# Gathering a block's tokens as 128 half rows instead of 64 whole rows, in a two-layer mixture-of-experts trunk

## What is computed

```
def expert_block(args):
    e, tok, g = args
    xb = ht[tok]
    hid = jax.nn.silu(xb @ w1[e]) * (xb @ w3[e])
    return (hid @ w2[e]) * g[:, None].astype(ht.dtype)
```

## Time and profile before

| | |
|---|---|
| median of 3 executions | 1592.72 us (1591.69 to 1592.96) |
| profiled execution | 1593.22 us |
| its span, first to last instruction | 1591.4 us |
| PE busy | 1360.1 us (85%) |
| DVE, ACT, POOL busy | 757.1, 508.5, 125.4 us |
| HBM read, written | 312.06 MB, 30.24 MB |
| expert stage of layer 0 | from 474 to about 872 us |
| expert stage of layer 1 | from 1239 to about 1555 us |

### The profile page before, as it was taken

One profiled execution on the slowest core, in us unless ns is written; L12 is line 12 of the kernel. 1 busy time (PEld: TensorE's weight loads), 2 busy tenths in 40 slices (PEclk: granted clock), 3 DMA queues, 4 the chain that ended last, 5 costly groups with the idle time before them and its releaser, 6 DMA issues. The chain is left out here.

```text
span 1591.4 us, 22877 instructions
## 1 busy us (share of the span) xinstructions
PE 1360.1 (85%) x6778; PEld 638.4 (40%) x6779; DVE 757.1 (48%) x1405; ACT 508.5 (32%) x783; POOL 125.4 (8%) x176
## 2 busy tenths in 40 slices
PE   4799998469968899999998399799897779989980
PEld 2555563224433333333332244388643323323330
DVE  2699999955764221222211542366547322232215
ACT  4101001043324443343322320166422253454422
POOL 0000000001221000101000200000002100000001
PEclk9899999789978999999999699799998899999995
DMA  9825464535059999899642500130094799999915
GB/s 345 286 70 204 146 258 176 206 116 203 27 207 372 375 371 344 277 303 343 204 142 95 213 0 0 30 77 2 19 365 166 261 336 384 366 378 375 353 33 191
DMA packets 163826, 342.97 MB, mean 216 GB/s; under 512 B 9104, under 2 KB 34304, under 8 KB 163776
## 3 DMA queue, kind: packets, MB, share of 16 engines
q1 hardware_dynamic: 146448, 298.29, 52.8%
q0 software_dynamic: 7440, 25.43, 5.2%
q10 hardware_dynamic: 9888, 18.62, 3.4%
HBM read 312.06 MB, written 30.24 MB: 215 GB/s over the span
## 5 line engine op out<-in xcount | busy, mean ns | idle before, releaser
L1480 PE MATMUL PS<-WR,XT 128*64 128x512 f32 x1760 | 414.4, 614 | 36.2 <-DVE WR L1613 26.5
L1480 PEld LDWEIGHTS PS<-WR,XT 128*64 128x64 f32 x1760 | 127.6, 141 | 273.2 <-issue 208.8
L1625 DVE TENSOR_TENSOR HID<-PS,SIL 64x512 f32<-64x512 f32 x55 | 37.6, 683 | 396.9 <-ACT SIL L1557 396.9
L1493 PE MATMUL PS<-WR,HTT 128*64 128x512 f32 x880 | 206.6, 613 | 9.5 <-ACT HTT L1562 9.5
L1546 ACT ACTIVATE WR<-WR 128x2048 f32 x90 | 169.0, 1906 | 107.8 <-issue 96.7
L1198 PE MATMUL PS<-HT,RING 128*128 128x512 f32 (+1 forms) x512 | 170.1, 496 | 8.5 <-DVEq L1296 8.4
L1613 DVE COPY WR<-WR 128x2048 f32 x90 | 107.1, 1224 | 114.6 <-DMA WR<-in_moe_w 51.3
L1198 PEld LDWEIGHTS PS<-HT,RING 128*128 128x128 f32 x512 | 100.0, 196 | 76.3 <-issue 68.4
L1318 DVE SCALAR_TENSOR_TENSOR AR<-AR,cols 128x783 f32 (+3 forms) x135 | 126.5, 937 | 0.0
L1318 DVE SCALAR_TENSOR_TENSOR ROWS<-AR,cols,ROWS 128x783 f32<-128x783 f32 (+2 forms) x126 | 118.0, 936 | 0.0
L1493 PEld LDWEIGHTS PS<-WR,HTT 128*64 128x64 f32 x880 | 59.6, 140 | 111.5 <-issue 108.0
(11 more groups left out here) (234 smaller groups left out, 1337.5 us busy)
## 6 DMA issues: line engine op xcount, KB each, us to landing
WR<-in_moe_w SPq DMA_DIRECT2D x192, 1024.0 KB, 15.1
RING<-in_w_mod SPq DMA_DIRECT2D x24, 2048.0 KB, 15.0
moe_out<-YO ACTq DMA_DIRECT2D x110, 128.0 KB
RING<-in_conv_pw SPq DMA_DIRECT2D x16, 512.0 KB, 5.4
moe_out<-HT SPq DMA_DIRECT2D x16, 512.0 KB, 8.4
ROWS<-rows_of_layer SPq DMA_DIRECT2D x12, 512.0 KB, 6.1
RING<-in_attn_w_qkv SPq DMA_DIRECT2D x3, 2048.0 KB, 8.6
RING<-in_conv_pw SPq DMA_DIRECT2D x2, 2048.0 KB, 9.9
```

The lines of the kernel that those rows point to most:

```text
L1480: ins = pe.matmul(PUV[g * SUB:(g + 1) * SUB, :], XT[:, k, :], w[:, k * FE:(k + 1) * FE], start=(k == 0), stop=(k == KT - 1), tile_position ...
L1493: ins = pe.matmul(PYO[c * SUB:(c + 1) * SUB, :], HTT[:, k, :], W2[:, at:at + 512], start=(k == 0), stop=(k == FE // P - 1), tile_position= ...
L1625: nc.vector.tensor_tensor(HID[:, :], PUV[0:SUB, :], SIL[:, :], ALU.mult).then_inc(hid_ready[L], 1)
```

## The change

A block's tokens are gathered as 128 half rows of 2 KB: the token table is read as rows of 512, the index of lane i is twice the token's number, and that of lane 64 + i one more. XG becomes 128 partitions x 512: partitions 0 to 63 hold the lower halves of the 64 tokens' rows, 64 to 127 the upper halves. For this `find` writes FOUND to all 128 partitions (each matmul twice, into the lower and upper half of the columns), BLOCK holds doubled token numbers (constant `tok2`), and DVE adds the constant `half` (0 or 1) as it casts FOUND to IDX. `turn_x` turns tile k from the lower half and tile k + 4 from the upper half, alternately, into their two banks; the eight results stand where they stood. The constants make CN seven columns wider, and XG takes half the bytes of each partition.

```
-            XG = shared("XG", [SUB, D])
+            XG = shared("XG", [P, D // 2])
...
-            src = h2d[L][:, :] if L == 0 else h2d[L][0:SEQ, :]
+            src = (h2d[L][:, :] if L == 0 else h2d[L][0:SEQ, :]).rearrange("t (h n) -> (t h) n", h=2)
             pool.indirect_dma_start(out=XG[:, :], out_offset=None, in_=src,
-                                    in_offset=bass.IndirectOffsetOnAxis(ap=icur[0:SUB, 0:1], axis=0)
+                                    in_offset=bass.IndirectOffsetOnAxis(ap=icur[:, 0:1], axis=0)
...
-            FOUND = PS[0:SUB, 0, 0:cells]
+            FOUND = PS[:, 0, 0:cells]
...
                     for q in range(q0, q1):
-                        ins = pe.matmul(FOUND, LANE[:, q, :], BLOCK[:, q, 0:cells],
-                                        start=(q == 0), stop=(q == 2 * NT - 1))
+                        for h in range(2):
+                            ins = pe.matmul(FOUND[h * SUB:(h + 1) * SUB, :], LANE[:, q, :], BLOCK[:, q, 0:cells],
+                                            start=(q == 0), stop=(q == 2 * NT - 1), tile_position=(0, h * SUB))
...
-                                           const("tokid")[:, u:u + 1], ALU.is_equal, ALU.mult)
+                                           const("tok2")[:, u:u + 1], ALU.is_equal, ALU.mult)
...
-                pool.tensor_copy(icur[0:SUB, :], IDX[0:SUB, 0:1]).then_inc(idx_first[L], 1)
+                pool.tensor_copy(icur[:, :], IDX[:, 0:1]).then_inc(idx_first[L], 1)
...
-                V_.tensor_copy(IDX[0:SUB, 0:cells], FOUND).then_inc(idx_ready[L], 1)
+                V_.tensor_scalar(IDX[:, 0:cells], FOUND, const("half"), None, ALU.add).then_inc(idx_ready[L], 1)
...
-                        for k in range(KT):
-                            ins = pe.transpose(PXT[k // 4][:, k % 4 * SUB:(k % 4 + 1) * SUB], XG[:, k * P:(k + 1) * P],
-                                               ident[0:SUB, 0:SUB])
+                        for k in range(KT // 2):
+                            for h in range(2):
+                                rows = slice(h * SUB, (h + 1) * SUB)
+                                ins = pe.transpose(PXT[h][:, k * SUB:(k + 1) * SUB], XG[rows, k * P:(k + 1) * P],
+                                                   ident[rows, rows])
```

More of the change, by code:

```diff
@@ L61 @@
 _at = 0
-for _n, _w in (("ident", P), ("tri", P), ("pick", 2), ("pick_e", NE), ("tokid", TILES), ("rev4", NG), ("rev16", NE),
+for _n, _w in (("ident", P), ("tri", P), ("pick", 2), ("pick_e", NE), ("tokid", TILES), ("tok2", TILES), ("half", 1), ("rev4", NG), ("rev16", NE),
                ("iota", DEEP_SUB[0] * NE), ("thr", DEEP_SUB[0]), ("swap", NE),
@@ L86, in constant_table @@
     put("tokid", i[:, None] + P * np.arange(TILES)[None, :])
+    put("tok2", 2 * (i[:, None] + P * np.arange(TILES)[None, :]))
+    put("half", (i >= SUB)[:, None])
     put("rev4", NG - np.arange(NG)[None, :])
@@ L173, in build @@
             HTT = shared("HTT", [P, FE // P, SUB])
-            shared("past_HT", [P, KT * TOK - 3328])
+            shared("past_HT", [P, KT * TOK - 2816])
             WR = shared("WR", [P, 9 * WSLOT])
@@ L1447, in _ @@
                         pool.wait_ge(info_ready[L], 1)
-                        pool.tensor_copy(icur[0:SUB, :], IDX[0:SUB, bass.ds(cell, 1)]).then_inc(idx_set[L], 1)
+                        pool.tensor_copy(icur[:, :], IDX[:, bass.ds(cell, 1)]).then_inc(idx_set[L], 1)
                         pool.wait_ge(info_ready[L], 1)
```

## The result

The changed kernel takes 1571.51 us (median; 1569.58 to 1573.51) beside 1592.8 for the kernel before: ratio 0.9863, 95% interval 0.9848 to 0.9878, so 21.3 us less. The forecast was 1584.5 us, 8.2 less; the gain is two and a half times that. The profiled execution took 1571.96 us, span 1570.2.

What follows compares the result with a forecast made beforehand. PE was taken to bound most blocks, saturated DMA layer 0 until 542 and layer 1 from 1276 to 1482. Turns -10.0 (7.6, 1.4, 1.0) plus costs 1.8 give -8.2 from 1592.7: 1584.5 us, range 1581 to 1594.6.

Steps and rivals of the forecast that it cites:

- The turns: Each block's eight turns: row halves overlap as four pairs, 0.2 us of steps instead of 0.49, gaining 0.28 us a block.
- ACT's chain: Blocks before a change of expert: x copy to W1's first half begins 0.28 us earlier, gain 0.26 a block.
- 7.6: Layer 0 from 541.8: 28 turns, 17 x 0.28 + 11 x 0.26 us gained.
- The 1.0 us for the three turns at layer 1's head: Three turns before 1276 pull the whole later transfer stream: 0.26 twice and 0.5 for the first.
- Pairs do not overlap: Rival: turns keep the 0.06 us pace at which instructions come, only costs are left, 1594.5 us; chance 0.13.
- ACT's chain stays: Rival: ACT's chain before a change of expert stays with SiLU, 3.2 us less gain, 1587.7 us; chance 0.13.
- Late gathers: Rival: doubled descriptors make 15 gathers land past their cover in blocks, +23 us, 1607.5 us; chance 0.08.
- 0.8 is left for 64 more rows: Gather landing: 0.8 us later for 64 more rows, judged from the combine's gathers; paid at each layer's head.
- The costs of 1.8 us: Two layers at 0.9 us each: 0.8 for the later gather, 0.1 for small edits to the index steps.
- Those of 1276 to 1482 drown in DMA: Layer 1's saturated stretch: time saved by faster turns there is lost waiting for weights, so no gain counted.
- the low end of the range, 1581.0: Gather cost at 0 and 0.35 us gained per turn: 1580.6, so the range starts from 1581.

Runs made afterwards that it cites:

- turns_only: Kernel before, 64 whole rows still gathered onto 64 partitions, with turns alternating between lower and upper half of the rows: 1585.48 us, 0.9951.
- address_only: Kernel before with only the two added constant columns, unread, so all tensors behind them start 32 bytes later: 1591.08 us, 0.9991.
- rows_on_64_127: Kernel before, its gather of 64 whole rows written to partitions 64 to 127 and the eight turns read from there: 1593.26 us, 0.9999.
- half_rows_old_turns: Changed kernel's gather of 128 half rows, but all eight turns read the lower 64 partitions as before the change: 1584.35 us, 0.9938.
- gather_only: Changed kernel with its turns reordered, four of the lower half of the rows, then four of the upper half: 1572.48 us, 0.9863.
- long_pieces: Changed kernel with weights in 8 KB runs per partition, the turns reading columns with a stride of four (two for hidden values): 1581.75 us, 0.9929.
- hidden_halves: Changed kernel with the hidden values also laid out in two halves of partitions, their four turns run as two pairs: 1568.62 us, 0.9838.
- long_pieces_dealt: Changed kernel with weights in 8 KB runs, VectorE dealing the features out so that PE reads 128 columns in a row: 1563.37 us, 0.9819.

## Why the prediction was wrong

- **The turns: right.** Overlap of the row halves, 0.46 us for 0.43, a gain of 0.25 a block for 0.28; ACT's chain moved with them (0.24 for 0.26). From turn 5 to 32 this gave 6.7 us for 7.6. The term was 0.03 a block too large: I divided 0.49 us into seven equal steps of 0.07. In the records the first step takes 0.11 and the others 0.063, before as after, so that three steps are 0.24 us and not 0.2. The 1.0 us for the three turns at layer 1's head is not shown: turns_only had 0.0 from 33 to 36, and 0.8 from 36 to 52, less than the 2.0 and 2.5 by which address_only and rows_on_64_127 differ there without faster turns.
- **The rivals.** Pairs do not overlap: refuted, eight records start within 0.24 us. The rule that was weighed for it (the Trainium skill, TensorE: Matmul & The Clock Gate, section "Wait — 56ns, not 53.3ns?", about 62 ns a matmul where they are decoded in firmware) would have needed seven steps, by estimate 0.43 us. It does not set the pace here; which way they are decoded no run shows. ACT's chain stays: refuted. Late gathers: no sign of it, landings became 0.7 us shorter instead of longer.
- **"0.8 is left for 64 more rows": wrong in sign.** The nearest row was that of the combine's gathers, which land later than the present one. They move twice the bytes, and I put what bytes at the full rate did not explain on the number of rows. At layer 1's head issue to turns became 1.0 us shorter, with the landing. In layer 0 it stayed (5.63 and 5.58): there the gather had landed 1.7 us (before) and 1.9 us (after) ahead of the turns, so that it did not decide. The costs of 1.8 us were not paid: DVE's index step grew by 0.07, 0.42 for 0.35, and PE's index product took 1.55 for 1.54. Layer 0's stage did begin 1.6 us later, but 1.5 of that is there by 330 us, before anything that the change touches, by a lower clock in an earlier stage (from 310 to 332 us the same 38 matmul records ran 14.20 us at a mean granted clock of 0.84 before, 16.43 us at 0.71 after).
- **"Those of 1276 to 1482 drown in DMA": the step that failed.** For the turns alone it holds: turns_only gained 0.8 us there and nothing in layer 0 before block 5. What failed is what it took for granted, that the stream's speed is that of the kernel before. I read 373 GB/s as the ceiling and looked at the gather's form only for its own landing, "the same bytes", and not for what it does to the transfers beside it. That is worth 9.2 us by the medians of half_rows_old_turns; in its profiled execution 3.7 stand in layer 0 and 6.0 in layer 1. No case of the forecast had it, and the low end of the range, 1581.0, allowed only for a gather cost of 0 and faster turns.
- **It could have been seen.** The gathers' total on the page, 25.43 MB with the combine's, doesn't tell, but in the saturated stretch their share is out of proportion to SP's: q0 7.0% for 3.93 MB is 3.7 us per MB, q1 2.74. And the Trainium skill's page on SBUF named above gives the rule; I had weighed only the page on TensorE.

## What to carry to other kernels

The same 256 KB took less DMA time on 128 partitions, or on 32 to 95, than on 0 to 63 or 64 to 127 (174 and 170 ns a record for 236 and 233). Where DMA is the bound, ask of each transfer, small ones too, which partitions it writes, and compare its time per byte with its neighbours'. If 64 are enough, 32 to 95 did as well here as all 128. A change to one engine's layout was two changes here, one for the engine and one for the queues that fill it; where a stretch was bound by DMA, only the second counted.

## What the runs showed that was not expected

- A gather on one half of the partitions slows the other queue's records: 126 ns for 90 on average, of 2 KB, while it runs. The gather was 7% of the DMA time in layer 1's saturated stretch, and its form was worth 9 us.
- Eight turns issued as four of the lower and four of the upper rows run in pairs all the same, 13 to 15 ns apart (gather_only). Here the alternate order need not have been written out by hand.
- Turns that read their 128 columns with a stride of four elements, or of two, cost 0.69 us for eight (and for four) instead of 0.46: the stride takes back what the row halves give. On VectorE a step of 128 x 1024 elements with a stride of four costs 2.04 us instead of 1.30.
- Weights in runs of 8 KB in place of 2 and 4 KB move at 402 GB/s (long_pieces, 476 to 535) where the short ones had 385 and 388 (the change, hidden_halves). In layer 1's saturated stretch it was 399 for 390; long_pieces_dealt, whose stream is less often the bound there (share 0.95), moved 389.
